# A gating unit's bias moved from TensorE to VectorE, with two prompt tiles in one product

## What is computed

```python
def sgu(u, v, w_s, b_s):
    b, t, _ = u.shape
    c = min(t, CHUNK)
    n = t // c
    tri = jnp.tril(jnp.ones((c, c), dtype=w_s.dtype))
    ws = w_s[:, :c, :c] * tri[None]
    vr = v.reshape(b, n, c, SGU_GROUPS, SGU_GROUP_DIM)
    mixed = jnp.einsum('gts,bnsgd->bntgd', ws, vr) + b_s[:, :c].T[None, None, :, :, None]
    return u * mixed.reshape(b, t, SGU_WIDTH)
```

## Time and profile before

| | |
|---|---|
| median of 3 runs | 1818.61 us (1816.3 to 1821.88) |
| profiled execution | 1824.75 us |
| its span in the trace | 1822.9 us |
| the stage of the change | about 795 to 906 us of the span |
| granted clock of TensorE, whole span | 0.909 |

### The profile page before, as it was taken

How to read it: one execution, slowest core, us unless ns; L and a number is a source line. 1 busy time by engine, 2 the same in 40 slices (tenths; PEclk the granted TensorE clock), 3 DMA queues, 4 the chain that set the end, 5 groups by cost and what they waited for, 6 DMA issues and landing times. The chain is left out here.

```text
span 1822.9 us, 17942 instructions
## 1 busy us (share of the span) xinstructions
PE 1580.0 (87%) x6826; PEld 813.4 (45%) x6826; DVE 384.5 (21%) x741; ACT 292.8 (16%) x619; POOL 78.1 (4%) x109
## 2 busy tenths in 40 slices
PE   7999999999999688879799999949789887899780
PEld 4444445555556555555344466423233332333230
DVE  2101000002321343455520022431010100101014
ACT  3000000113221122234510022200000000000001
POOL 0000000001000000000000000000101010011000
PEclk9999999999999699976889999959988898899985
DMA  8464226242310444400093322478998999899955
GB/s 324 173 281 145 93 90 215 99 151 99 133 58 1 148 130 142 134 24 0 28 311 129 148 80 106 147 303 358 387 409 337 395 404 382 357 390 413 406 213 200
DMA packets 113800, 380.16 MB, mean 209 GB/s; under 512 B 17459, under 2 KB 55387, under 8 KB 83047
## 3 DMA queue, kind: packets, MB, share of 16 engines
q1 hardware_dynamic: 108050, 343.27, 50.1%
q0 software_dynamic: 5552, 27.89, 4.5%
q10 hardware_dynamic: 144, 8.26, 1.1%
HBM read 390.41 MB, written 26.49 MB: 229 GB/s over the span
## 5 line engine op out<-in xcount | busy, mean ns | idle before, releaser
L2187 PE MATMUL bank<-W,hT_e 128*64 128x512 f32 x576 | 276.0, 635 | 55.3 <-DMA w_u<-in_w_exp_up 54.2
L2188 PE MATMUL bank<-w_u,hT_e 128*64 128x512 f32 x576 | 276.0, 635 | 0.0
L2187 PEld LDWEIGHTS bank<-W,hT_e 128*64 128x64 f32 x576 | 81.9, 146 | 243.7 <-issue 165.5
L2204 PE MATMUL bank<-W,actT 128*64 128x512 f32 x576 | 149.8, 680 | 9.0 <-ACT actT L2215 9.0
L489 PE MATMUL bank<-raw,hT 128*128 128x512 f32 (+1 forms) x320 | 134.1, 581 | 0.6 <-PEq L242 0.6
L720 PE MATMUL bank<-subT,w 128*128 128x504 f32 (+1 forms) x320 | 132.5, 544 | 0.0
L489 PE MATMUL bank<-w_in,hT 128*128 128x512 f32 (+2 forms) x320 | 123.7, 547 | 0.0
L1581 PE MATMUL bank<-W,mixT 128*128 128x512 f32 x256 | 113.7, 605 | 1.6 <-DVE mixT L1802 1.6
L489 PEld LDWEIGHTS bank<-raw,hT 128*128 128x128 f32 x320 | 62.4, 197 | 69.2 <-issue 68.9
L2204 PEld LDWEIGHTS bank<-W,actT 128*64 128x64 f32 x576 | 45.3, 156 | 100.4 <-issue 94.8
L489 PEld LDWEIGHTS bank<-w_in,hT 128*128 128x128 f32 x320 | 60.4, 190 | 61.0 <-issue 61.0
(11 more groups left out here) (371 smaller groups left out, 1683.1 us busy)
## 6 DMA issues: line engine op xcount, KB each, us to landing
W<-in_w_exp_down SPq DMA_DIRECT2D x76, 1024.0 KB, 22.2
W<-in_w_exp_gate SPq DMA_DIRECT2D x72, 1024.0 KB
w_u<-in_w_exp_up SPq DMA_DIRECT2D x72, 1024.0 KB
raw<-in_w_in SPq DMA_DIRECT2D x3, 4096.0 KB
W<-in_w_out SPq DMA_DIRECT2D x3, 4096.0 KB, 13.6
w_in<-in_w_in SPq DMA_DIRECT2D x2, 4096.0 KB, 14.6
k_in<-in_cache_sel_k SPq DMA_DIRECT2D x64, 128.0 KB, 2.1
v_in<-in_cache_sel_v SPq DMA_DIRECT2D x64, 128.0 KB, 2.4
```

The lines of the kernel that those rows point to most:

```text
L2187: pe.matmul(bank[4 + u][0:NS, :], hT[:, u, c, :], w_g[:, c, :], start=(c == 0), stop=(c == KC - 1))
L2188: mm = pe.matmul(bank[4 + u][UP, :], hT[:, u, c, :], w_u[:, c, :], start=(c == 0), stop=(c == KC - 1))
L2204: mm = pe.matmul(bank[2 * u + n // 2][lane, :], actT[:, q, :], w_d[:, u, q, 512 * n:512 * n + 512], start=(q == 0), stop=(q == 3))
```

## The change

In the prompt, one product now makes a group of both tiles: the 128x128 matrix is loaded once and 2 x 128 columns of values go through it, into 256 columns of a PSUM bank. A part (`mix_part`) has two such groups, so that parts 0 to 3 are all the 8 groups of both tiles. Parts 4 and 5 are four groups of the samples each, as before. The products that spread the bias are gone from all parts. The bias is turned once instead: two small products in `spread` bring it into PSUM as columns (one value for each token and group), and `block_weights` copies them to `b_rows` and to the end of `rep`. VectorE's fused operation `scalar_tensor_tensor` then adds the bias as a value for each partition and multiplies by `u`: two instructions of 256 columns in parts 0 to 3, four of 128 columns in parts 4 and 5. The copy that makes `b_new` moves from step 2 to step 0 in DVE's queue.

```diff
--- before.py
+++ after.py
@@ -1141,7 +1141,8 @@
             bd = qr_flat[0:NS, 0:SG * NS].rearrange("p (g b t) -> p g b t", g=SG, b=NB)
             b_s = sb(scope, "b_s", [SG, P])
             b_new = sb(scope, "b_new", [SG, NS])
-            rep = sb(scope, "rep_s", [NS, SG * NT])
+            rep = sb(scope, "rep_s", [NS, SG * NT + SG])
+            b_rows = sb(scope, "b_rows", [P, SG])
             ws_loaded, ws_turned, masked, rep_made, bd_ready, mixed, gated = (sem("sgu_" + x) for x in (
                 "ws_loaded", "ws_turned", "masked", "rep_made", "bd_ready", "mixed", "gated"))
             pT = sb(scope, "p_pT", [P, 2, 2, 2, 2, NJ, P])
@@ -1158,6 +1159,7 @@
 
             STEPS = [(r, c, j) for r in range(2) for c in range(2) for j in range(NJ)]
             N = len(STEPS)
+            GATE_BANK = [5, 4, 4, 5, 4, 5]
 
             GROUPS = []
             for n, (r, c, j) in enumerate(STEPS):
@@ -1238,16 +1240,16 @@
                         mm.then_inc(ws_turned, 1)
 
                     def spread():
-                        pe.wait_ge(masked, 2)
-                        pe.matmul(bank[5][0:NS, 0:SG * NT].rearrange("p (g t) -> p g t", g=SG), cst("rep")[0:NT, :], wsT[0:NT, :, 0:NT],
-                                  start=True, stop=True).then_inc(rep_made, 1)
-
-                    GATE_BANK = [5, 4, 4, 5, 4, 5]
-
-                    def mix_half(k):
-
-                        r, m = k // 2, k % 2
-                        rows, to = (P if r < 2 else NS), bank[GATE_BANK[k]]
+                        pe.wait_ge(masked, 3)
+                        n = SG * NT
+                        pe.matmul(bank[5][0:NS, 0:n].rearrange("p (g t) -> p g t", g=SG), cst("rep")[0:NT, :], wsT[0:NT, :, 0:NT],
+                                  start=True, stop=True)
+                        pe.matmul(bank[5][0:NS, n:n + SG], b_new[:, :], ident[0:SG, 0:SG], start=True, stop=True)
+                        pe.matmul(bank[5][:, n + SG:n + 2 * SG], b_s[:, :], ident[0:SG, 0:SG], start=True, stop=True).then_inc(rep_made, 1)
+
+                    def mix_part(k):
+
+                        to = bank[GATE_BANK[k]]
                         pe.wait_ge(masked, 2)
                         pe.wait_ge(c_centred, 1)
                         pe.wait_ge(bd_ready, 1)
@@ -1257,12 +1259,16 @@
                             pe.wait_ge(o_kept, (k - 1) // 2)
                         if k == 4:
                             pe.wait_ge(placed, 1)
-                        b_of = b_s[:, :] if r < 2 else b_new[:, :]
-                        for i in range(4):
-                            g, part = 4 * m + i, to[0:rows, P * i:P * i + P]
-                            pe.matmul(part, b_of, ident[0:SG, g:g + 1].to_broadcast([SG, P]), start=True, stop=False)
-                            lhsT = wsT[:, g, :] if r < 2 else bd[:, g].rearrange("p b t -> p (b t)")
-                            mm = pe.matmul(part, lhsT, Z[0:rows, r, C_V + P * g:C_V + P * g + P], start=False, stop=True)
+                        if k < 4:
+                            for i in range(2):
+                                g = 2 * k + i
+                                mm = pe.matmul(to[:, 256 * i:256 * i + 256].rearrange("p (r d) -> p r d", r=2), wsT[:, g, :],
+                                               Z[:, 0:2, C_V + P * g:C_V + P * g + P], start=True, stop=True)
+                        else:
+                            for i in range(4):
+                                g = 4 * (k - 4) + i
+                                mm = pe.matmul(to[0:NS, P * i:P * i + P], bd[:, g].rearrange("p b t -> p (b t)"), Z[0:NS, 2, C_V + P * g:C_V + P * g + P],
+                                               start=True, stop=True)
                         mm.then_inc(mixed, 1)
 
                     scores(0)
@@ -1286,7 +1292,7 @@
                         if n == 1:
                             spread()
                         if n in (2, 3, 5, 7, 9, 11):
-                            mix_half((2, 3, 5, 7, 9, 11).index(n))
+                            mix_part((2, 3, 5, 7, 9, 11).index(n))
                         if n >= 4 and n % 4 == 0:
                             weighted(n // 4 - 1)
                         if n >= 4 and n % 4 == 2:
@@ -1403,20 +1409,31 @@
                         dve.tensor_tensor(wsT[:, 4 * m:4 * m + 4, :], bank[(5, 7)[m]].rearrange("p (g t) -> p g t", g=4),
                                           cst("tri").unsqueeze(1).to_broadcast([P, 4, P]), ALU.mult).then_inc(masked, 1)
 
+                    def spread_bias():
+                        dve.wait_ge(ws_loaded, 32)
+                        dve.tensor_copy(b_new[:, :].rearrange("p (b t) -> p b t", b=NB), b_s[:, 0:NT].unsqueeze(1).to_broadcast([SG, NB, NT])).then_inc(masked, 1)
+
                     def block_weights():
-                        dve.wait_ge(ws_loaded, 32)
-                        dve.tensor_copy(b_new[:, :].rearrange("p (b t) -> p b t", b=NB), b_s[:, 0:NT].unsqueeze(1).to_broadcast([SG, NB, NT]))
+                        n = SG * NT + SG
                         dve.wait_ge(rep_made, 1)
-                        own.link(dve.tensor_copy(rep[:, :], bank[5][0:NS, 0:SG * NT]))
+                        dve.tensor_copy(b_rows[:, :], bank[5][:, n:n + SG])
+                        own.link(dve.tensor_copy(rep[:, :], bank[5][0:NS, 0:n]))
                         dve.tensor_tensor(bd, cst("same_b", to="p (b t) -> p b t", b=NB)[0:NS].unsqueeze(1).to_broadcast([NS, SG, NB, NT]),
-                                          rep[:, :].rearrange("p (g t) -> p g t", g=SG).unsqueeze(2).to_broadcast([NS, SG, NB, NT]), ALU.mult).then_inc(bd_ready, 1)
-
-                    def gate_half(k):
-                        r, m = k // 2, k % 2
-                        rows = P if r < 2 else NS
+                                          rep[:, 0:SG * NT].rearrange("p (g t) -> p g t", g=SG).unsqueeze(2).to_broadcast([NS, SG, NB, NT]), ALU.mult).then_inc(bd_ready, 1)
+
+                    def gate_part(k):
                         dve.wait_ge(mixed, k + 1)
-                        dve.tensor_tensor(mix[0:rows, r, SW + 512 * m:SW + 512 * m + 512], bank[(5, 4, 4, 5, 4, 5)[k]][0:rows, :],
-                                          Z[0:rows, r, C_U + 512 * m:C_U + 512 * m + 512], ALU.mult).then_inc(gated, 1)
+                        held = bank[GATE_BANK[k]]
+                        for i in range(2 if k < 4 else 4):
+                            if k < 4:
+                                g = 2 * k + i
+                                made, rows, tiles, bias = held[:, 256 * i:256 * i + 256].rearrange("p (r d) -> p r d", r=2), slice(0, P), slice(0, 2), b_rows[:, g:g + 1]
+                            else:
+                                g = 4 * (k - 4) + i
+                                made, rows, tiles, bias = held[0:NS, P * i:P * i + P].unsqueeze(1), slice(0, NS), slice(2, 3), rep[:, SG * NT + g:SG * NT + g + 1]
+                            ins = dve.scalar_tensor_tensor(out=mix[rows, tiles, SW + P * g:SW + P * g + P], in0=made, scalar=bias,
+                                                           in1=Z[rows, tiles, C_U + P * g:C_U + P * g + P], op0=ALU.add, op1=ALU.mult)
+                        ins.then_inc(gated, 1)
 
                     take(0)
                     take(1)
@@ -1427,10 +1444,11 @@
                             compressed()
                             mask_weights(0)
                             mask_weights(1)
+                            spread_bias()
                         if n == 2:
                             block_weights()
                         if n in (3, 4, 6, 8, 10, 12):
-                            gate_half((3, 4, 6, 8, 10, 12).index(n))
+                            gate_part((3, 4, 6, 8, 10, 12).index(n))
                         weigh(n)
                         if n == 0:
                             compressed_weights()
```

## The result

The changed kernel takes 1803.14 us (median, 1797.96 to 1804.19) against 1820.24 (1816.3 to 1822.23) for the kernel before on the same chip: a ratio of 0.9878, with a 95% interval of 0.9854 to 0.9902. It is faster by 1.2%; the forecast was 0.7%.

A forecast was written before the change was run, and what follows sets the result against it. TensorE was taken to bound the stage, in a chain with VectorE. 1.15 - 7.73 + 0.46 - 4.0 = -10.1 us, with -2.8 for the clock about -13, gave 1805.6 us against 1818.6; range 1799.5 to 1811.5.

The forecast's parts named there:

- What bounds the stage: Steps 2 and 3: a closed chain over TensorE and VectorE; no transfers under way, so the stage's gain is the program's.
- TensorE's parts: First two parts, steps 2 and 3: each falls from about 5.79 to 1.92 us, saving 7.73 us together (5.8 to 8.7).
- The gates: Six VectorE gates: two operations 0.84 us, four 1.14, so 1.98 us added in all; 1.25 by the skill's fixed cost.
- The new small work: Two products in `spread`, the bias-column copy and the moved `b_new` copy: +1.15 us together (0.6 to 1.5).
- The later waits: VectorE's waits of 1.42, 1.26, 1.41 and 1.41 us at the four later gates go entirely; -4.0 us after dearer gates.
- The clock: Steps 6 to 12: the upper clock throughout would give about 5.6 us; half of the drops vanish, -2.8 us.
- rival (b): The clock goes up with the first weighted product and stays: -16.6 us, 1802 us; chance 0.17.
- Rival (c): Less work between the gaps never releases the clock before the stage's end: +9 us, 1827.6 us; chance 0.03.
- Rival (d): VectorE or ScalarE also bound steps 2 and 3, so the wait stays: gain under 5 us, 1814 to 1820; chance 0.07.

The follow-up runs named there:

- e12: Changed kernel with the last four gates moved from VectorE to ScalarE (bias) and GpSimd (multiply), second run of this version: 1799.41 us, ratio 0.9878.
- e5: Kernel before the change, nothing removed, its 8 bias rows padded with zeros to 128 rows: 1802.93 us, ratio 0.9882.
- e3: Changed kernel with an extra 8-row product of 256 columns ahead of each prompt product, in turn, overwritten: 1813.20 us, ratio 0.9958.
- e4: Changed kernel with an extra 128-row product of 256 columns ahead of each prompt product, in turn, overwritten: 1800.28 us, ratio 0.9909.
- e8: Changed kernel with the last four gates moved from VectorE to ScalarE (bias) and GpSimd (multiply), first run of this version: 1803.09 us, ratio 0.9881.
- e9: Changed kernel with four extra 8-row products of 128 columns in a row ahead of each prompt part, overwritten: 1811.61 us, ratio 0.9948.
- e10: Changed kernel with two extra 8-row products of 256 columns in a row ahead of each prompt part, overwritten: 1812.36 us, ratio 0.9940.

## Why the prediction was off

**What bounds the stage** was right. The chain over TensorE and VectorE in steps 2 and 3 was there, the gain fell into this stage, and none was given back behind it.

**TensorE's parts.** 1.92 us forecast at the lower clock; 1.78 measured, with the clock up at its end, and 1.84 in e12 (825.15 - 823.31), where the whole part ran at that clock. The price was right, the reason for its lower bound not: the 0.72 us of the earlier trace rows was taken as the price of a 128-column product, and e5 shows that such a product takes 0.43 at that clock when its neighbours use as many rows. For the same reason a part before is 3.33 us at the upper clock and not the 2.9 that the forecast took. The second part ran at the upper clock (0.95).

**The gates.** 0.84 us forecast for two operations, 0.80 to the next start measured (822.36 - 821.56); 1.14 for four, 1.03 (854.98 - 853.95). That is 4 x 0.19 + 2 x 0.42 = 1.6 us for the six, between the 1.98 of the forecast's terms and its other estimate, 1.25. (The bounds that it gives for them, 0.6 and 3.4, come out of its own terms as 0.9 and 3.6.) **The new small work:** 1.15 forecast; the transposes of step 2 came 0.85 us later in the stage (24.41 us after its start against 23.56). **The later waits** went, all four. (Of the prices for the clock, the 1.09 us for two groups of transposes stands in the earlier trace rows with x4; the changed kernel shows all eight in 1.09 us, at 851.44, so it was read rightly.)

So the work, with the second part still priced at the lower clock, is 0.85 - (5.79 - 1.84) - (5.78 - 1.84) + 2 x 0.19 for the first two gates, and -5.50 + 2 x 0.19 + 2 x 0.42 for the later four: -10.9 us, where -10.1 was forecast.

**The clock** is the step that failed: "I expect about half of the drops to vanish: -2.8 us". The stage lost 17.1, so 6.2 are left for the clock, a remainder and not a measurement of its own. They divide at the scores of step 8, which stand in step 5: they came 9.7 us sooner, against 6.7 of work up to there (-0.85 + 3.95 + 3.94 - 0.38), and that leaves 3.1 us; behind them it is the other 3.1 (7.4 less 4.3 of work). The second half is the term as forecast: four stretches at the lower clock (20 us in all) became two (7 us). The first half was missing altogether: the forecast let the clock stay low through steps 2 to 5, and rival (b) let it rise only "with the first weighted product". It rose a step and a half before that. The total lies at rival (b)'s -16.6, but by another way than (b)'s: the clock rose earlier and didn't stay up throughout (0.93 over 838.7 to 885.8):

```profile
838.70:885.80 47.10, 36.85 (x192) 18.42 (x190) 32.07 (x51) 26.95 (x80) 0.00 (x0) 0.93 0.00 1
```

The prediction had the right sentence for it, that what goes out "are products with 8 rows of the array in use, which fill TensorE's queue and use little of it", and stopped at a guess of half. Its rows held a hint of more: 36 of 44 us busy without once going up say that something in that work is not what raises the clock, and all of its parts 0 and 1 were products in turn with 8-row ones. But it was only a hint, since ahead of those parts the clock is low in the changed kernel too.

The split into 10.9 us of work and 6.2 of clock also holds for one order only. e5 leaves all the work in and gains 17.5 us, and against it the change's fewer products gain nothing (93.1 us against 92.7). Much of what was priced as work removed, 0.72 us a product, was the cost of standing in turn with 8 rows. So the forecast took for two independent terms what is largely one cause.

Rival (c), that less work between the gaps keeps the clock down, fell: the changed kernel is less busy and has the higher clock, and the Trainium skill's statement (TensorE: Matmul & The Clock Gate, Part 1) that activity releases the throttle agrees with e3 and e4 only if activity isn't busy time (14.18 us busy at 0.50, 12.24 at 1.00). Rival (d) fell for steps 2 and 3; but VectorE is the late engine at the later gates, as e8 and e12 show at three of the four (0.73 to 0.78 us less each).

The time itself, 1803.14 us, lies within the range of 1799.5 to 1811.5. But the kernel before measured 1820.24 here and not the 1818.6 from which the range was made. As ratios the range is 0.9895 to 0.9961 and the forecast 0.9929, and the measured 0.9878 lies beyond its fast end; the two repeats, 0.9902 and 0.9897, lie just inside. That the absolute time fell into the range is luck in part. The three agree that the gain is larger than forecast, though the interval of the first repeat (to 0.9934) still takes in the 0.9929.

**What stays open:** where between 8 and 128 rows the clock's behaviour turns, whether the padding helps through the array's rows or through the operands' partitions read, why some short rises come without a difference in the code, and why a change of row count costs 0.3 us for each product.

## What to carry to other kernels

Look at the granted clock in each stretch beside TensorE's busy share. Where TensorE is busy and the clock is low, look for products with few rows in use among full ones: pad them with zeros to 128 rows (two clears and no other work here, for 17.5 us of this stage), or move what they do to another engine. If they must stay, put them together rather than in turn with full ones: that saves the changes of row number (2.00 us for four in a row against 2.9), but it did not bring the clock up here. When a wait has been removed, ask which engine is late at that place now, and give its work to one that has time: that was worth 1.7 to 1.8 us of stage more by itself, and 3.6 to 4.0 with what the clock did in those traces. Before a few microseconds are put down to a change, compare the steps between the same two instructions at the same granted clock.

## What the runs showed of the hardware that was not expected

- The clock follows the rows in use: products of equal columns and count kept it at the lower level for 17 us longer with 8 rows than with 128 (up at 45.6 us in e3, at 28.6 in e4; with the same columns in other orders at 45.5 in e9 and e10), though TensorE was busy for 14.18 of 16 us. The padded rows of e5 are zeros, so nonzero values in them aren't needed.
- A 128-column fp32 product takes 0.43 us at the lower clock and 0.225 at the upper among products of equal rows, and 0.72 where 8-row and 128-row products stand in turn; a product of 8 rows among its like takes the same 0.43 (e9), and each change of the row number costs 0.29 us at the lower clock; with 256 columns 0.86 and 0.43 (e4), in turn 1.15 at the lower (e3).
- A fused operation of VectorE with a value for each partition costs 0.40 us to the next start for 256 columns out of PSUM, and 0.26 for 128 (1.03 / 4).
- ScalarE adds a bias to 2 x 256 columns out of PSUM in 0.81 us, and GpSimd multiplies 512 columns in SBUF in 1.27 us, while VectorE's own work beside them goes on as before (1.22 us for 1024 columns).
